# Retention heads: the 80 tail tokens' value block first, state growths among the second z projection

## The chip, the cores and the metric

The kernel runs on one core of a Trainium2 chip. The metric is the device time of one execution in microseconds (us), the median of several runs. One execution was also profiled; every duration below is from it.

## What is computed

One inference step of a two-layer trunk on 528 prompt tokens (16 of them meta tokens) and 8 sample sequences of 8 tokens. Each layer has a retention branch of four heads, a gated recurrent branch, gates and an output projection. The change lies in the retention heads alone:

```python
def retention_chunk(q, k, v, S, log_g):
    ...
    scores = jnp.einsum('blhd,bmhd->bhlm', q, k) * decay[None]
    inner = jnp.einsum('bhlm,bmhe->blhe', scores, v)
    cross = jnp.einsum('blhd,bhde->blhe', q, S) * cross_decay[None, :, :, None]
    S_new = jnp.exp(log_g * L)[None, :, None, None] * S + jnp.einsum(
        'blhd,blhe->bhde', k * state_decay[None, :, :, None], v)
    return inner + cross, S_new
```

Each sample sequence has its own state S (256x512 in f32, 512 KB) per head and layer, which is read, used for `cross`, grown by its 8 tokens and written back.

## The kernel before, in words

The 592 tokens are cut into four blocks of 128 and a tail of 80 (`TAIL`: 16 prompt tokens and the 64 sample tokens). Every matmul in full precision is made of three products of a high and a low part, so each operand is split: ScalarE (ACT) copies the rounded high part (`w_hi`, `vtok_hi`), VectorE (DVE) subtracts to get the low part (`w_lo`, `vtok_lo`).

All engines run programs written out by hand and meet at semaphores. Weights come in units of 512 KB over a ring of four slots: SyncE (SP) issues unit u when unit u - 4 is used up (`unit_done`), ACT and DVE split it (`split_hi`, `split_lo`, lines 398 and 406) three units ahead of its use. Results go to four PSUM banks in turn (`bank`), which ACT or DVE free; the tail's value block has a bank of its own (`v_last`), the samples' output too (`o_last`).

TensorE (PE) runs, for each head: four projections for q and k (units 0 to 3); `values(0)` to `values(3)` (units 4 to 7), each adding two of the eight 128-row steps to all five token blocks of v; between them `keys` (transposes of k) and `cross(0)`, the queries of the first four sample sequences times their states; the z projections `proj 8` and `proj 9`; the score products (five jobs); then `grow(0, 0)`, half of `proj 10`, `grow(0, 1)`, the other half, `grow(1, 0)`; `inner` (four token blocks, 30 matmuls) with `grow(1, 1)` after its second block; the tail's part of the output; `prompt_state(0)`, `cross(1)` with the other four states, `prompt_state(1)`; transposes of the normalised output; `proj 11`; and the product with w_a (units 12 to 15), among which `grow_four` grows the other four states.

`grow(pair, c)` (PE line 1485) makes the new part of two states' half c, from `kst` and `vst`, the stacks of high and low parts of the samples' keys and values. DVE adds it to the decayed state (line 924), and after c = 1 tells POOL (`s_upd`), which stores the two states (line 517), waits for each store to land and loads the next sequence's state into its place (line 512). `cross(1)` waits for these loads.

The stacks go through HBM. In `stacks` SP waits for the split keys (`ktok_ready`), writes them to `k_scr` (three DMAs, line 443), reads them back as `kst` and `kst3` (lines 445, 446), waits for all values (`vtok_ready`), writes `v_scr` (three DMAs, line 449), reads `vst` and `vst3` (lines 451, 452), and waits until everything has landed (`st_in`) before it issues the next weight unit. It does all this behind the load of unit 11. PE waits for `st_in` ahead of `grow(0, 0)`.

In the heads each engine's loop over units i says where its steps stand: DVE updates states at the end of i = 9 and in i = 10, and after the first block's variance.

Of the kernel before, what the change touches and what calls it, by code (L numbers as in the profile page):

```python
# [33 lines left out]
P = 128  # L34
# [8 lines left out]
TB = 5  # L43
# [15 lines left out]
RAW = 4  # L59

# [86 lines left out]
def phases():  # L147
# [3 lines left out]
    r += [(("apart", u), 1) for u in range(3)] + [(("v", j), 0) for j in range(4)] + [(("apart", 3), 1)]  # L151
# [32 lines left out]
def trunk(nc, x_in, w_units, gate_w, packs, final_gain, consts, decay, state_ret,  # L184
# [7 lines left out]
    with ctx:  # L192
# [107 lines left out]
        def sem(name):  # L300
# [20 lines left out]
            "vth_ready", "scm_ready", "sch_ready", "zero_ready", "rest_ready", "scr_in", "st_in"))  # L321
        zt_ready, ktok_ready, vtok_ready, sc_ready = (sem(n) for n in (
# [90 lines left out]
        def _(sp):  # L413
# [24 lines left out]
            def stacks(l, h):  # L438

                hh = l * HEADS + h  # L440
                sp.wait_ge(ktok_ready, hh + 1)
                for n, src in enumerate((ktok_hi, ktok_lo, ktok_hi)):
                    sp.dma_start(k_scr[:, n], src[0:TAIL, 4, :].bitcast(f32)).then_inc(scr_in, 16)
                sp.wait_ge(scr_in, 48 + hh * 96 + 48)
                sp.dma_start(kst[:, :, :].bitcast(f32), stacked(k_scr)).then_inc(st_in, 16)
                sp.dma_start(kst3[0:STACK * TAILP, :].bitcast(f32), k_scr[0:2].rearrange("s p r e -> (s p r) e"))                    .then_inc(st_in, 16)
                sp.wait_ge(vtok_ready, hh + 1)
# [4 lines left out]
                sp.dma_start(vst3[0:STACK * TAILP, :].bitcast(f32), v_scr[0:2].rearrange("s p r e -> (s p r) e"))                    .then_inc(st_in, 16)  # L452
                sp.wait_ge(st_in, hh * 64 + 64)
# [4 lines left out]
            for u in range(RING, UNITS):  # L458
# [11 lines left out]
                if at < HEADS * 16 and at % 16 == 11:  # L470
                    stacks(l, at // 16)
# [9 lines left out]
        def _(pool):  # L481
# [13 lines left out]
            for l in range(0, DEPTH):  # L495
# [7 lines left out]
                for h in range(0, HEADS):  # L503
# [18 lines left out]
                    pool.memset(vst3[STACK * TAILP:P, :].bitcast(f32), 0.0).then_inc(rest_ready, 1)  # L522
# [63 lines left out]
        def _(act):  # L586
# [48 lines left out]
            for l in range(0, DEPTH):  # L635
# [9 lines left out]
                for h in range(0, HEADS):  # L645
# [10 lines left out]
                    for i in range(11):  # L656
# [17 lines left out]
                        if i == 7:  # L674
                            for j in range(TB):
                                if j < 4:
                                    wait_job(act, "R", l, h, ("v", j))
                                else:
                                    wait_job(act, "R", l, h, ("apart", 3))
                                act.activation(vtok_hi[0:BLK[j], j, :], v_bank(j)[0:BLK[j], :], ACT.Copy)\  # L680
                                   .then_inc(vth_ready, 1)
# [1114 lines left out]
```

## Time and profile before

| | |
|---|---|
| runs | 2088.36, 2089.3, 2093.83 us |
| median | 2089.3 us |
| the profiled execution's own time | 2092.4 us |
| its span from the first to the last instruction | 2090.5 us |
| PE busy | 2026.7 us, 97% |
| DVE, ACT, POOL busy | 57%, 34%, 8% |
| mean granted clock of TensorE | 0.993 |

A stage is measured as a stretch of PE's timeline from its first matmul to the first matmul of the next stage. Busy time of PE does not tell a wait exactly, since matmuls are pipelined and their ends are modelled. A row of the windows view begins with the stretch and its length in us, then busy time and instruction count of each engine, then the granted clock, the DMA share and GB/s; its last row sums all stretches asked for. A row of the timeline is start, duration, engine, line, what is written and read, and in brackets the idle time before it. PEld is the loading of weights into the array, which overlaps PE.

The eight heads are the four heads of layer 0 and the four of layer 1. The fourth head is the last of layer 0; its `values(2)` starts at 497.79 us.

### The profile page before, as it was taken

Reading aid. Unit: us, or ns where it says so; the run is one execution under the profiler, and the core shown is the slowest. Engines: PE = TensorE matmul, PEld = TensorE weight load, DVE = VectorE, ACT = ScalarE, POOL = GpSimd, SP = SyncE. Lnnn points to the kernel's source line nnn. Section 1 sums busy time; section 2 is a strip of 40 time slices with the busy share of each in tenths; the row PEclk is TensorE's granted clock in tenths of the full one; section 3 lists DMA queues with packets and bytes.
Section 4 is the critical chain, followed back from the end, with each engine's and each line's share of the span. In section 5 each row is a group of like instructions: output and inputs, shape, how many; then the busy total and the mean of one; then the engine's idle time right before and its main releaser. Section 6 shows DMA issues by size and latency. Waiting matters only on the chain.

```text
span 2090.5 us, 32504 instructions
## 1 busy us (share of the span) xinstructions
PE 2026.7 (97%) x13512; PEld 1866.9 (89%) x13512; DVE 1186.9 (57%) x2021; ACT 715.2 (34%) x1110; POOL 161.5 (8%) x222
## 2 busy tenths in 40 slices
PE   8999999899999999999999999999999999999998
PEld 7878888798799999999987887987987999999997
DVE  7655455464567776424584554645645677753345
ACT  4322222222226665422332222222122366654222
POOL 1020120120200000000001201202102000000000
PEclk9999999999999999999999999999999999999999
DMA  5334443442442212222244334424433422132222
GB/s 206 101 124 159 145 142 97 153 163 85 143 152 84 74 66 101 93 80 72 91 157 152 128 101 154 167 82 148 152 104 127 156 79 79 61 117 81 71 90 79
DMA packets 100833, 241.43 MB, mean 115 GB/s; under 512 B 8622, under 2 KB 48286, under 8 KB 100302
## 3 DMA queue, kind: packets, MB, share of 16 engines
q1 hardware_dynamic: 78446, 149.78, 21.8%
q0 software_dynamic: 22240, 89.57, 12.0%
q8 instruction: 107, 1.75, 0.3%
q14 instruction: 40, 0.33, 0.1%
HBM read 190.13 MB, written 49.18 MB: 114 GB/s over the span
## 4 chain that ended last, share of the span: by engine, by line
PE 66%; DMA 12%; DVE 11%; ACT 3%; DVEq 3%; issue 2%; SPq 2%; ACTq 1%; POOL 1%; POOLq 0%
PE bank L1391 15%; PE bank L1393 15%; PE bank L1392 15%; PE bank L1454 5%; PE bank L1456 4%; PE bank L1455 4%; DMA out_ret_s<-S 4%; DMA w_raw<-in_w_units 2%; PE o_last L1470 2%; DVE w_lo L406 2%; DMA S<-in_state_ret 2%; DVE rr L1273 2%; DVE ct L1211 1%; DMA vst<-v_scr 1%; DVEq L927 1%
## 5 line engine op out<-in xcount | busy, mean ns | idle before, releaser
L1391 PE MATMUL bank<-xn_hi,w_hi 128*128 128x296 f32 x2432 | 728.5, 300 | 6.2 <-DVE w_lo L406 4.9
L1393 PE MATMUL bank<-xn_lo,w_hi 128*128 128x296 f32 x2432 | 726.7, 299 | 0.0
L1392 PE MATMUL bank<-xn_hi,w_lo 128*128 128x296 f32 x2432 | 723.6, 298 | 0.0
L1391 PEld LDWEIGHTS bank<-xn_hi,w_hi 128*128 128x128 f32 x2432 | 457.4, 188 | 12.5 <-DVE w_lo L406 8.0
L1392 PEld LDWEIGHTS bank<-xn_hi,w_lo 128*128 128x128 f32 x2432 | 458.1, 188 | 0.3
L1393 PEld LDWEIGHTS bank<-xn_lo,w_hi 128*128 128x128 f32 x2432 | 456.2, 188 | 0.0
L406 DVE TENSOR_TENSOR w_lo<-w_raw,w_hi 128x1024 fp32r<-128x1024 f32 x245 | 299.1, 1222 | 250.7 <-ACT w_hi L398 244.0
L398 ACT ACTIVATE w_hi<-w_raw 128x1024 fp32r<-128x1024 f32 x245 | 258.5, 1055 | 456.2 <-DMA w_raw<-in_w_units 451.6
L1391 PE MATMUL bank<-oa_hi,w_hi 128*128 128x296 f32 x512 | 154.0, 301 | 0.0
L1393 PE MATMUL bank<-oa_lo,w_hi 128*128 128x296 f32 x512 | 153.2, 299 | 0.0
L1392 PE MATMUL bank<-oa_hi,w_lo 128*128 128x296 f32 x512 | 152.9, 299 | 0.0
L1393 PE MATMUL bank<-ob_lo,w_hi 128*128 128x296 f32 x384 | 115.1, 300 | 0.0
L1391 PE MATMUL bank<-ob_hi,w_hi 128*128 128x296 f32 x384 | 114.5, 298 | 0.0
L1392 PE MATMUL bank<-ob_hi,w_lo 128*128 128x296 f32 x384 | 114.2, 297 | 0.0
L1454 PE MATMUL bank<-w_hi,xn_hi 128*128 128x512 f32 x256 | 102.8, 402 | 2.9 <-DVE rot_k L966 1.4
L1391 PEld LDWEIGHTS bank<-oa_hi,w_hi 128*128 128x128 f32 x512 | 96.3, 188 | 5.8 <-issue 5.8
L1456 PE MATMUL bank<-w_lo,xn_hi 128*128 128x512 f32 x256 | 101.0, 394 | 0.0
L1455 PE MATMUL bank<-w_hi,xn_lo 128*128 128x512 f32 x256 | 100.8, 394 | 0.0
L1392 PEld LDWEIGHTS bank<-oa_hi,w_lo 128*128 128x128 f32 x512 | 96.3, 188 | 0.0
L1393 PEld LDWEIGHTS bank<-oa_lo,w_hi 128*128 128x128 f32 x512 | 96.3, 188 | 0.0
L517 POOL DMA_DIRECT2D out_ret_s<-S x64 | 45.7, 717 | 463.3 <-DVEq L927 291.5
L946 DVE SCALAR_TENSOR_TENSOR zz<-zz,bank 128x296 f32<-128x296 f32 x64 | 29.5, 461 | 83.8 <-ACT zz L653 81.9
(233 smaller groups left out, 3162.5 us busy)
## 6 DMA issues: line engine op xcount, KB each, us to landing
w_raw<-in_w_units SPq DMA_DIRECT2D x216, 512.0 KB, 3.3
S<-in_state_ret POOLq DMA_DIRECT2D x64, 512.0 KB, 4.8
out_ret_s<-S POOLq DMA_DIRECT2D x64, 512.0 KB, 6.0
w_raw<-in_w_units SPq DMA_DIRECT2D x64, 256.0 KB, 3.2
gw<-in_gate_w POOLq DMA_DIRECT2D x8, 896.0 KB, 4.8
vst<-v_scr SPq DMA_DIRECT2D x8, 512.0 KB, 4.1
out_ret_p<-Sp POOLq DMA_DIRECT2D x8, 512.0 KB, 4.0
v_scr<-vtok_hi SPq DMA_DIRECT2D x16, 160.0 KB
```

The source lines that it names most:

```text
L398: act.activation(w_hi[:, n % RING, :], w_raw[:, n % RING, :], ACT.Copy).then_inc(unit_hi, 1)
L406: dve.tensor_tensor(w_lo[:, n % RING, :], w_raw[:, n % RING, :], w_hi[:, n % RING, :].bitcast(f32), SUB).then_inc(unit_lo, 1)
L517: pool.dma_start(dst, S[:, s, :, :]).then_inc(s_out[s], 16)
L946: dve.scalar_tensor_tensor(zz[:, i - 8, a:b], zz[:, i - 8, a:b], 1.0, psum_of("R", name)[:, 0:HALF], ADD, MUL)\
L1273: dve.tensor_tensor_scan(rr[:, t, :], aa[:, t, :], ii[:, t, :], 0.0, MUL, ADD)
L1391: pe.matmul(ps, w_hi[:, slot, cols], x_hi, start=first, stop=False)
L1392: pe.matmul(ps, w_lo[:, slot, cols], x_hi, start=False, stop=False)
L1393: return pe.matmul(ps, w_hi[:, slot, cols], x_lo, start=False, stop=last)
L1454: pe.matmul(ps, left_hi, right_hi, start=first, stop=False)
L1455: pe.matmul(ps, left_lo, right_hi, start=False, stop=False)
L1456: return pe.matmul(ps, left_hi, right_lo, start=False, stop=last)
L1470: ins = pe.matmul(o_last[at:at + QUAD, :], qz[:, c, b * QUAD:b * QUAD + QUAD], S[:, s, c, :], start=(n < 4 and c == 0), stop=(n >= 4 and c ...
```

## The change

The tail's value block is computed first within each `values(u)` (`VALUE_ORDER`), and signals `v_tail_full` by itself. ACT and DVE split it ahead of the others and ahead of unit 10's split. SP's `stacks` is cut into three: `key_rows` behind the issue of unit 9, `key_stack` and `value_stack` behind that of unit 10, and SP no longer waits for the landing (the next head's `key_rows` does). PE waits for `st_in` ahead of `proj 9`. The growths stand: (0, 0) before `proj 9`, (0, 1) between its halves, (1, 0) behind it and ahead of the scores, (1, 1) behind the scores and ahead of `proj 10`. DVE's updates follow them. PE's wait for POOL's memset (`rest_ready`) moves to the tail's output.

```diff
+VALUE_ORDER = (4, 0, 1, 2, 3)
...
-            def stacks(l, h):
-
-                hh = l * HEADS + h
+            def key_rows(hh):
+
                 sp.wait_ge(ktok_ready, hh + 1)
+                if hh:
+                    sp.wait_ge(st_in, hh * 64)
                 for n, src in enumerate((ktok_hi, ktok_lo, ktok_hi)):
                     sp.dma_start(k_scr[:, n], src[0:TAIL, 4, :].bitcast(f32)).then_inc(scr_in, 16)
+
+            def key_stack(hh):
...
-                sp.wait_ge(vtok_ready, hh + 1)
+            def value_stack(hh):
+
+                sp.wait_ge(v_tail_ready, hh + 1)
...
-                sp.wait_ge(st_in, hh * 64 + 64)
...
-                if at < HEADS * 16 and at % 16 == 11:
-                    stacks(l, at // 16)
+                if at < HEADS * 16:
+                    hh = l * HEADS + at // 16
+                    if at % 16 == 9:
+                        key_rows(hh)
+                    elif at % 16 == 10:
+                        key_stack(hh)
+                        value_stack(hh)
...
+                        if i == 7:
+                            act.wait_ge(v_tail_full, hh + 1)
+                            act.activation(vtok_hi[0:TAIL, 4, :], v_last[0:TAIL, :], ACT.Copy).then_inc(vth_ready, 1)
                         split_hi(act, "R", l, h, i)
...
+                        if i == 7:
+                            dve.wait_ge(vth_ready, hh * TB + 1)
+                            dve.tensor_tensor(vtok_lo[0:TAIL, 4, :], v_last[0:TAIL, :],
+                                              vtok_hi[0:TAIL, 4, :].bitcast(f32), SUB).then_inc(v_tail_ready, 1)
                         if i != 9:
                             split_lo(dve, "R", l, h, i)
...
                     project("R", l, h, ("proj", 8), 8)
-                    project("R", l, h, ("proj", 9), 9)
+                    pe.wait_ge(st_in, hh * 64 + 64)
+                    pe.wait_ge(kt_free, hh * 3 + 3)
+                    grow(0, 0)
+                    project("R", l, h, ("proj", 9), 9, (0,))
+                    grow(0, 1)
+                    project("R", l, h, ("proj", 9), 9, (1,))
+                    grow(1, 0)
                     pe.wait_ge(qkl_ready, hh + 1)
...
-                    pe.wait_ge(st_in, hh * 64 + 64)
-                    pe.wait_ge(rest_ready, hh + 1)
-                    pe.wait_ge(kt_free, hh * 3 + 3)
-                    grow(0, 0)
-                    project("R", l, h, ("proj", 10), 10, (0,))
-                    grow(0, 1)
-                    project("R", l, h, ("proj", 10), 10, (1,))
-                    grow(1, 0)
+                    grow(1, 1)
+                    project("R", l, h, ("proj", 10), 10)
...
-                        if i == 1:
-                            grow(1, 1)
                     pe.wait_ge(ktok_ready, hh + 1)
+                    pe.wait_ge(rest_ready, hh + 1)
```

SP's queue before, in the first head, from the load of unit 8 (the first row is units 8 to 11); `w_raw` are weights, `k_scr` and `v_scr` the scratch in HBM, `kst` and `vst` the stacks (with a number: `kst3`, `vst3`):

```order
L469 DMA w_raw<-in_w_units 128x1024 x4
L443 DMA k_scr<-ktok_hi 10x8x256
L443 DMA k_scr<-ktok_lo 10x8x256
L443 DMA k_scr<-ktok_hi 10x8x256
L445 DMA kst<-k_scr 128x2x256
L446 DMA kst_81<-k_scr 64x256
L449 DMA v_scr<-vtok_hi 10x8x512 x2
L449 DMA v_scr<-vtok_lo 10x8x512
L451 DMA vst<-v_scr 128x2x512
L452 DMA vst_95<-v_scr 64x512
L469 DMA w_raw<-in_w_units 128x1024 x8
```

And SP's queue after the change, at the same place:

```order
L479 DMA w_raw<-in_w_units 128x1024 x2
L446 DMA k_scr<-ktok_hi 10x8x256
L446 DMA k_scr<-ktok_lo 10x8x256
L446 DMA k_scr<-ktok_hi 10x8x256
L479 DMA w_raw<-in_w_units 128x1024
L451 DMA kst<-k_scr 128x2x256
L452 DMA kst_81<-k_scr 64x256
L459 DMA v_scr<-vtok_hi 10x8x512 x2
L459 DMA v_scr<-vtok_lo 10x8x512
L461 DMA vst<-v_scr 128x2x512
L462 DMA vst_95<-v_scr 64x512
L479 DMA w_raw<-in_w_units 128x1024 x9
```

The key writes moved ahead of unit 10, the two stacks ahead of unit 11.

DVE before, from the split of unit 11 (`w_lo`) to the first state update (`S`); `zz` is z, `sc` the scores:

```order
L406 TENSOR_TENSOR w_lo<-w_raw,w_hi 128x1024
L946 SCALAR_TENSOR_TENSOR zz<-zz,bank 128x296 x2
L1033 MEMSET sc 128x64 x3
L1034 MEMSET sc 128x192
L1041 TENSOR_TENSOR sc<-bank,dec 128x264 x2
L1041 TENSOR_TENSOR sc<-bank,dec 128x400
L1041 TENSOR_TENSOR sc<-bank,dec 128x272
L1041 TENSOR_TENSOR sc<-bank,dec 128x144
L1046 TENSOR_TENSOR sc<-bank,cst 80x16
L1048 TENSOR_TENSOR sc<-bank,cst 80x4x16
L924 SCALAR_TENSOR_TENSOR S<-S,cst,sums 128x512 x2
L1056 TENSOR_TENSOR sc_lo<-sc,sc_hi 128x1600
```

And DVE after the change, from the same split:

```order
L408 TENSOR_TENSOR w_lo<-w_raw,w_hi 128x1024
L940 SCALAR_TENSOR_TENSOR S<-S,cst,sums 128x512 x2
L962 SCALAR_TENSOR_TENSOR zz<-zz,bank 128x296
L940 SCALAR_TENSOR_TENSOR S<-S,cst,sums 128x512 x2
L962 SCALAR_TENSOR_TENSOR zz<-zz,bank 128x296
L940 SCALAR_TENSOR_TENSOR S<-S,cst,sums 128x512 x2
L1052 MEMSET sc 128x64 x3
L1053 MEMSET sc 128x192
L1060 TENSOR_TENSOR sc<-bank,dec 128x264 x2
L1060 TENSOR_TENSOR sc<-bank,dec 128x400
L1060 TENSOR_TENSOR sc<-bank,dec 128x272
L1060 TENSOR_TENSOR sc<-bank,dec 128x144
```

Three of the four pairs of state updates now stand ahead of the scores, the fourth behind them.

## Rows read from the trace of the kernel before

**Rows 1.** The page, part 1: busy us, share of the span, instructions.
```profile
PE 2026.7 (97%) x13512; PEld 1866.9 (89%) x13512; DVE 1186.9 (57%) x2021; ACT 715.2 (34%) x1110; POOL 161.5 (8%) x222
```

**Rows 2.** Who waited for whom: us in total, times, longest us.
```profile
DVE vo L1078 <- POOL rstd_gn L492: 53.7, 8, 8.0
...
PEld o_last L1470 <- DMA S<-in_state_ret: 36.3, 16, 4.7
...
PE o_last L1470 <- DMA S<-in_state_ret: 20.6, 14, 3.8
...
PEld sums L1485 <- DVE S L924: 15.7, 16, 1.7
```

**Rows 3.** Windows, cross(1) in the eight heads (third head, sum): stretch, length, busy, clock.
```profile
406.29:415.36 9.07, 5.29 (x17) 0.86 (x17) 1.91 (x4) 0.60 (x1) 2.47 (x3) 0.81 0.37 117
...
sum 61.10, PE 40.51 PEld 6.26 DVE 15.31 ACT 4.78 POOL 13.29; mean PE 5.06 PEld 0.78 DVE 1.91 ACT 0.60 POOL 1.66
```

**Rows 4.** Windows, cross(0) in the eight heads: first head, and the sum.
```profile
59.14:60.99 1.85, 1.85 (x17) 0.42 (x16) 1.49 (x2) 0.81 (x1) 0.00 (x0) 1.00 0.51 168
...
sum 14.84, PE 14.84 PEld 3.35 DVE 12.65 ACT 8.75 POOL 0.00; mean PE 1.85 PEld 0.42 DVE 1.58 ACT 1.09 POOL 0.00
```

**Rows 5.** Windows, prompt_state(1) in the eight heads: the sum.
```profile
sum 24.32, PE 24.32 PEld 19.56 DVE 8.24 ACT 4.78 POOL 4.45; mean PE 3.04 PEld 2.45 DVE 1.03 ACT 0.60 POOL 0.56
```

**Rows 6.** Windows, prompt_state(0) in the eight heads: the sum.
```profile
sum 22.57, PE 22.57 PEld 16.54 DVE 0.00 ACT 0.00 POOL 6.45; mean PE 2.82 PEld 2.07 DVE 0.00 ACT 0.00 POOL 0.81
```

**Rows 7.** Windows, second half of proj 10 in the eight heads: the sum.
```profile
sum 33.16, PE 28.18 PEld 26.32 DVE 31.60 ACT 5.55 POOL 0.00; mean PE 3.52 PEld 3.29 DVE 3.95 ACT 0.69 POOL 0.00
```

**Rows 8.** Windows, first half of proj 10 in the eight heads: the sum.
```profile
sum 27.68, PE 27.68 PEld 26.36 DVE 17.36 ACT 20.35 POOL 0.00; mean PE 3.46 PEld 3.30 DVE 2.17 ACT 2.54 POOL 0.00
```

**Rows 9.** Windows, first nine matmuls of inner in the eight heads: the sum.
```profile
sum 24.26, PE 18.88 PEld 12.90 DVE 22.48 ACT 11.80 POOL 11.49; mean PE 2.36 PEld 1.61 DVE 2.81 ACT 1.47 POOL 1.44
```

**Rows 10.** Windows, fourth head: values(3), proj 8, scores, growth (0,0) with half a projection.
```profile
504.79:511.80 7.01, 7.01 (x32) 5.42 (x31) 2.13 (x3) 3.01 (x5) 0.00 (x0) 1.00 0.24 75
511.80:518.32 6.52, 6.52 (x49) 6.52 (x49) 2.55 (x5) 1.01 (x2) 0.00 (x0) 1.00 0.46 137
...
524.84:529.28 4.44, 4.44 (x38) 4.39 (x37) 2.68 (x9) 0.42 (x1) 0.00 (x0) 1.00 0.53 179
529.28:533.17 3.89, 3.89 (x27) 3.48 (x26) 2.24 (x6) 2.69 (x3) 0.00 (x0) 1.00 0.37 146
```

**Rows 11.** Timeline of SP's queue, fourth head: start, us, what is issued.
```profile
517.48 1.54 SPq L449 DMA_DIRECT2D v_scr<-vtok_hi  x2
...
522.51 0.50 SPq L452 DMA_DIRECT2D vst<-v_scr  x1
526.65 0.83 SPq L469 DMA_DIRECT2D w_raw<-in_w_units  x2
```

**Rows 12.** Timeline of ACT, fourth head: tail's high part, split of units 11 and 12.
```profile
512.00 0.59 ACT L680 ACTIVATE vtok_hi<-v_last 80x512 fp32r<-80x512 f32 x1 [0.41 <-PE v_last L1456]
...
518.84 1.05 ACT L398 ACTIVATE w_hi<-w_raw 128x1024 fp32r<-128x1024 f32 x1
...
530.11 1.06 ACT L398 ACTIVATE w_hi<-w_raw 128x1024 fp32r<-128x1024 f32 x1 [4.65 <-DMA w_raw<-in_w_units]
```

**Rows 13.** Timeline of DVE, fourth head: tail's low part, split of unit 11, growth (0,1)'s update.
```profile
513.21 0.68 DVE L1026 TENSOR_TENSOR vtok_lo<-v_last,vtok_hi 80x512 fp32r<-80x512 f32 x1
...
519.92 1.23 DVE L406 TENSOR_TENSOR w_lo<-w_raw,w_hi 128x1024 fp32r<-128x1024 f32 x1 [0.48 <-ACT w_hi L398]
...
536.51 1.40 DVE L924 SCALAR_TENSOR_TENSOR S<-S,cst,sums 128x512 f32<-128x512 f32 x2
```

**Rows 14.** Timeline of POOL: memset of the first head, stores of the third and fourth.
```profile
66.75 0.52 POOL L522 MEMSET vst<- 64x512 f32 x1 [42.10 <-DVEq L1021]
...
397.66 1.43 POOL L517 DMA_DIRECT2D out_ret_s<-S  x2
...
538.57 1.44 POOL L517 DMA_DIRECT2D out_ret_s<-S  x2 [37.10 <-DVEq L927]
```

More of the change, by code:

```diff
@@ L150, in phases @@
         r += halves(("proj", t), 1)
-    r += [(("apart", u), 1) for u in range(3)] + [(("v", j), 0) for j in range(4)] + [(("apart", 3), 1)]
+    r += [(("apart", u), 1) for u in range(3)] + [(("v", j), j // 3) for j in range(4)]
     for t in range(8, 11):
@@ L321, in trunk @@
             "vth_ready", "scm_ready", "sch_ready", "zero_ready", "rest_ready", "scr_in", "st_in"))
+        v_tail_full, v_tail_ready = sem("v_tail_full"), sem("v_tail_ready")
         zt_ready, ktok_ready, vtok_ready, sc_ready = (sem(n) for n in (
@@ L451, in stacks @@
                 sp.dma_start(vst[:, :, :].bitcast(f32), stacked(v_scr)).then_inc(st_in, 16)
[L452 to L453 removed]
+                sp.dma_start(vst3[0:STACK * TAILP, :].bitcast(f32), v_scr[0:2].rearrange("s p r e -> (s p r) e"))\
+                    .then_inc(st_in, 16)
             def stacked(scr):
@@ L521, in _ @@
                     pool.wait_ge(ktok_ready, hh + 1)
-                    pool.memset(vst3[STACK * TAILP:P, :].bitcast(f32), 0.0).then_inc(rest_ready, 1)
+                    pool.memset(vst3[STACK * TAILP:P, :].bitcast(f32), 0.0)
+                    pool.drain().then_inc(rest_ready, 1)
                     for pair in range(S_RING // PAIRED):
@@ L674, in _ @@
                         if i == 7:
[L675 to L680, printed above, removed]
+                            for j in VALUE_ORDER[1:]:
+                                wait_job(act, "R", l, h, ("v", j))
+                                act.activation(vtok_hi[:, j, :], v_bank(j)[:, :], ACT.Copy)\
                                    .then_inc(vth_ready, 1)
@@ L1022, in _ @@
                         if i == 7:
[L1023 to L1029 removed]
+                            for n, j in enumerate(VALUE_ORDER[1:]):
+                                dve.wait_ge(vth_ready, hh * TB + (n + 2))
+                                dve.tensor_tensor(vtok_lo[:, j, :], v_bank(j)[:, :], vtok_hi[:, j, :].bitcast(f32),
+                                                  SUB).then_inc(freed("R", ("v", j)), 1)
                             dve.drain().then_inc(vtok_ready, 1)
                         if i == 9:
+                            grow(1, 0)
                             for j in range(3):
@@ L1089, in gate @@
                                                         MUL, MUL)
-                    variance(0, False)
-                    grow(1, 1)
-                    for j in range(1, 4):
+                    for j in range(4):
                         variance(j, j == 3)
@@ L1505, in values @@
                         wait_unit("R", l, h, 4 + u)
-                        for j in range(TB):
+                        for j in VALUE_ORDER:
                             rows = BLK[j]
@@ L1513, in values @@
                                 k = 2 * u + i
-                                if h == 0 and j == 0:
+                                if h == 0 and j == VALUE_ORDER[0]:
                                     pe.wait_ge(xn_ready, l * KT + k + 1)
@@ L1520, in values @@
                                 done("R", ("v", j), ins)
-                        done("R", ("apart", u), ins)
+                            elif u == 3:
+                                ins.then_inc(v_tail_full, 1)
+                        if u < 3:
+                            done("R", ("apart", u), ins)
                     raw = (xg_hi, xg_lo)
```

19 lines of the change are left out of this document (6 added, 13 removed).

## The prediction

> **What bounds the kernel now.** I read the page's busy times first: TensorE (PE) is busy for 97% of the span [rows 1]. So only what makes PE wait, or makes its instructions longer, can be won. The list of waits [rows 2] names the waits of PE and of its weight loads (PEld; both wait at once, so their figures are not added): cross(1), the second half of the products with the sample states (line 1470), waits for reloaded states (S<-in_state_ret), and the growth products (line 1485) wait for VectorE's update of the states (line 924). Both stand in the retention heads, eight of them. To size them I compared stretches of the timeline that hold the same work: from the first matmul of a stage to the first matmul of the next.
>
> The 16 matmuls of cross(1) take 61.10 us over the eight heads [rows 3], the 16 of cross(0), whose states are there long before, 14.84 us [rows 4]: **46.3 us** of waiting. In the third head the stretch is 9.07 us at a granted clock of 0.81, so part of it ran at the lower of TensorE's levels (1.2 of 2.4 GHz) after PE had idled. The 12 matmuls of prompt_state(1) behind cross(1) take 24.32 us [rows 5], the same 12 of prompt_state(0) ahead of it 22.57 us [rows 6]: **1.7 us**, the same low clock running on. The second half of the third z projection takes 33.16 us [rows 7], the first half 27.68 us [rows 8]: **5.5 us**, since growth (1,0) behind it waits for VectorE. The first nine matmuls of inner, up to growth (1,1), take 24.26 us [rows 9]; at 22.57/96 = 0.235 us a matmul 72 of them are 16.9 us, and a restart behind a growth costs about 0.1 each (0.8): **6.5 us** of waiting for VectorE. Together 60.0 us, 7.5 a head. That is the most that the change can find in these places.
>
> **The change, part by part.** I place its steps in the fourth head, where values(3) runs 504.79 to 511.80 and the first z projection 511.80 to 518.32 [rows 10].
>
> Tail block first. In values(3) the 80 tail tokens are six of 30 matmuls: 7.01/5 = 1.4 us, so they are done at 506.2 instead of 511.8. ScalarE copies them in 0.59 [rows 12], VectorE subtracts in 0.68 [rows 13]: v_tail_ready comes at about 507.6. Both engines were waiting for unit 10's weights there, so nothing stands behind. The four other blocks end up to 1.4 us later each; the first of them is due only when the first z projection starts, and ScalarE reaches it behind the same weights as before. Cost 0.
>
> The stack. From the first v_scr issue (517.48) to the landing of the whole stack, which SP waited for before it issued the next weights (526.65), it takes 9.2 us [rows 11]. Starting at 507.6 it is there at **516.8**. PE now asks for it behind the first z projection, at 518.3: 1.5 us to spare, cost 0. The three key writes go out earlier, between two weight loads, and SP no longer sits on the landing, so units 12 and 13 are issued as soon as their slots are free. In the first head of a layer the keys are late: its values(2) starts at 60.99 [rows 4], the memset that waits for the same signal runs at 66.75 [rows 14], 5.8 us in; three issues of some 0.75 [rows 11] end at 8.1, while unit 10's slot is free at 7.0. Unit 10 is 1.1 us late in two heads; between nothing and 1.1 reaches PE each time, I take 0.6: **1.2 us** in all. (The value stack still meets its time: it waits for the tail block, not for the keys.)
>
> Growths. Their number is the same; each costs PE its pair of matmuls and a restart, wherever it stands. New is what VectorE has in hand there. It splits unit 11 at 519.92 for 1.23 [rows 13], and only then makes growth (0,0)'s update, two instructions of 1.40 together [rows 13]: done at 522.55. A growth with the half projection behind it takes 3.89 [rows 10], of which the half alone is 27.68/8 = 3.46 [rows 8] and the pair 0.43; so PE comes to growth (0,1) at 518.32 + 3.89 = 522.2. It waits 0.35, in eight heads **2.8 us**. Growth (0,1)'s and (1,0)'s updates then have 3.5 us of projection each as cover against 1.40 of work; (1,1)'s runs while PE is in the whole third projection (6.5 us), and so does the scores' split. The scores' five products need a bank back from VectorE, behind (1,0)'s update; bounds are 0 and the 1.40 of that update; I take 0, as four banks are free for the first four jobs.
>
> The reloads. PE's times run on: score (4.44 [rows 10]) ends at about 531.4, growth (1,1) and the third projection at 538.5, inner (30 matmuls of 0.235) at 545.6, tail and prompt_state(0) at 552.3. Growth (1,1)'s update is done near 533.7; the first store of the pair before followed 0.66 behind the update (536.51 + 1.40 to 538.57 [rows 13, 14]), so the last two stores start at 534.4. The longest way from there to the end of cross(1) was the third head's: 397.66 [rows 14] to 415.36 [rows 3], 17.7 us. Even so it would end at 552.1, before cross(1) could end undisturbed (552.3 + 1.85). So the 46.3 and the 1.7 go wholly. With the wait gone, nothing idles PE and the clock stays at its upper level.
>
> The Trainium skill, "TensorE: Matmul & The Clock Gate" (section on the HAM clock gate), says that the slow state is the default and activity lifts it; by it the 1.7 us goes only if no wait of like length takes the place of this one, and without that rule I would leave it in: 2035.0 instead of 2033.3.
>
> What is late next: the transposes behind prompt_state(1) need VectorE's normalised blocks, which today wait for a POOL instruction (53.7 us over eight heads [rows 2]) that stands behind the reload issues. These are over 10 us earlier, so it is free when the variances are.
>
> **Sum.** 60.0 - 2.8 - 1.2 = 56.0 us. The profiled execution took 2092.4 us (span 2090.5) and would take 2036.4; it lies 3.1 above the median, so against the median of 2089.3 I forecast **2033.3 us**, 2.7% less.
>
> **Rivals.**
> - VectorE or ScalarE late in the second projection. Unit 11's load now goes out behind the stack's transfers. If it only starts when they land, it is there at 516.8 + 3.46 (526.65 issued, 530.11 used [rows 11, 12]) = 520.3, and ScalarE wants it at 518.84 [rows 12]: 1.4 us later for VectorE and for growth (0,1), 11 us in all: **2044.5**. The same comes of a bank that comes back 1.4 us late in the scores. For it: everything there hangs on one chain. Against it: SP issues it at 513, and a load needs no more than that 3.46 where nothing is ahead. Chance 0.11.
> - The reloads still collide. Stores and reloads now run beside units 13 and 14. If they take a further 3.4 us (one such load) over the longest way above, cross(1) ends at 555.5 instead of 554.2, 1.3 us a head: **2043.7**. The Trainium skill, "DMA: Bandwidth & Descriptors" (section "Issuing engines are not separate DMA queues"), states that transfers issued from all engines interleave on the same 16 DMA engines, which speaks for it. Against it: the way above is already the longest of the eight, and it held the same kind of company. Chance 0.05.
> - The wait moves to the transposes. If the POOL instruction were late for another reason, the 46.3 would return there: **2079.6**. Against it: its cause is the issue order, which changes. Chance 0.04, half of it within 0.3%.
> - Slower than before. PE now needs the stack 11 us earlier. Each microsecond over 1.5 is paid in every head. If the writes and reads, queued behind unit 10's load and the key stack, took twice their 9.2 us, PE would wait 7.7 us a head, 61.6 in all against the 56.0: **2094.9**; it decides at 17.7 us for the stack. Against it: the 9.2 us were themselves taken behind a weight load and the key stack. Chance 0.03.
>
> **How the numbers follow.** Forecast 0.77. Faster by over 0.3% (about what a measurement of this kernel can tell from no change): 0.77 + 0.11 + 0.05 + 0.02 = 0.95; within: 0.02; slower: 0.03. The range reaches from the whole 60.0 us won, with some 2 us for the runs' spread and a first values block that waits less (2027), to the first two rivals (2045).
>
> **What would show it.** cross(1) near 1.86 us a head and no wait for S<-in_state_ret at all; granted clock 1.00 there. The second half of the third projection like the first, inner 30 matmuls in 7.0 us without a gap. A wait of the growth for line 924's successor of about 0.35 us a head, and none for the stack. PE over 99% busy. If the stretch between the first z projection and the growth shows PE waiting for vst or kst, the stack's term is wrong; if cross(1) still waits, the reloads' is.

## The result and the profile after

| | before | after |
|---|---|---|
| median of the runs | 2089.95 us | 2033.96 us |
| runs from, to | 2088.36 to 2093.83 | 2033.44 to 2036.12 |
| span of the profiled execution | 2090.5 us | 2034.3 us |
| mean granted clock of TensorE | 0.993 | 0.999 |

The ratio of the times is 0.9731, with a 95% interval of 0.9715 to 0.9748: 2.7% faster. The forecast was 2033.3 us. The page, part 1, has PE at 98% of the span with 28.4 us less of busy time than in [rows 1], for the same 13512 matmuls: in the kernel before, waiting also showed as busy time, because the ends of matmuls are modelled, and some matmuls were slow.

```profile
PE 1998.3 (98%) x13512; PEld 1864.3 (92%) x13512; DVE 1187.1 (58%) x2021; ACT 715.6 (35%) x1110; POOL 161.5 (8%) x222
```

The waits of PE alone, three of the seven that the view lists (against [rows 2]; columns: us in total, times, longest). The seven come to 26.5 us; the four left out are 4.9, 4.4, 2.1 and 1.1. The wait for reloaded states (S<-in_state_ret) is gone altogether:

```profile
PE bank L1406 <- DVE w_lo L888: 9.4, 1, 9.4
...
PE v_last L1469 <- DVE xn_lo L927: 3.5, 4, 1.4
...
PE sums L1500 <- DVE S L940: 1.1, 3, 0.6
```

The last of these is the growths' wait for VectorE (now line 940). In the kernel before, PE's own row for it was:

```profile
PE sums L1485 <- DVE S L924: 10.4, 15, 1.3
```

The same stretches as in [rows 3 to 9], in the windows view (stretch, length, busy time and count of PE, PEld, DVE, ACT and POOL, granted clock, DMA share, GB/s). cross(1), third head and the sum of eight; then the sum of prompt_state(1):

```profile
395.26:397.12 1.86, 1.86 (x18) 0.42 (x17) 0.00 (x0) 0.60 (x1) 0.00 (x0) 1.00 0.02 4
...
sum 14.86, PE 14.86 PEld 3.36 DVE 0.00 ACT 4.78 POOL 0.00; mean PE 1.86 PEld 0.42 DVE 0.00 ACT 0.60 POOL 0.00
...
sum 23.19, PE 23.19 PEld 18.47 DVE 8.25 ACT 4.78 POOL 4.45; mean PE 2.90 PEld 2.31 DVE 1.03 ACT 0.60 POOL 0.56
```

The first half of proj 9, now behind growth (0, 0): first, third and fourth head, and the sum. A half without a wait takes 3.46, so the sum holds 30.13 - 27.68 = 2.4 us of waiting:

```profile
82.81:86.69 3.88, 3.54 (x26) 3.30 (x24) 3.00 (x4) 1.47 (x3) 0.00 (x0) 1.00 0.40 135
...
361.51:365.65 4.14, 3.54 (x26) 3.30 (x24) 3.05 (x5) 1.58 (x3) 0.00 (x0) 1.00 0.35 127
500.57:504.25 3.68, 3.54 (x28) 3.30 (x26) 3.00 (x4) 1.16 (x3) 0.00 (x0) 1.00 0.39 142
...
sum 30.13, PE 28.30 PEld 26.42 DVE 24.08 ACT 10.05 POOL 0.00; mean PE 3.54 PEld 3.30 DVE 3.01 ACT 1.26 POOL 0.00
```

And three more sums of eight: the second half of proj 9, proj 10 whole, inner whole (30 matmuls):

```profile
sum 27.68, PE 27.68 PEld 26.32 DVE 13.05 ACT 0.00 POOL 8.85; mean PE 3.46 PEld 3.29 DVE 1.63 ACT 0.00 POOL 1.11
...
sum 53.00, PE 53.00 PEld 53.00 DVE 41.77 ACT 17.25 POOL 17.17; mean PE 6.62 PEld 6.62 DVE 5.22 ACT 2.16 POOL 2.15
...
sum 55.56, PE 55.56 PEld 45.14 DVE 36.66 ACT 24.38 POOL 11.43; mean PE 6.95 PEld 5.64 DVE 4.58 ACT 3.05 POOL 1.43
```

In each of the three PE's busy time equals the length, and the lengths are those of undisturbed work (3.46 us a half; the forecast had 7.0 for inner, and it takes 6.95): nothing is waited for.

What the first half of proj 9 waits for stands in the timelines of ACT and then of DVE, fourth head (idle time before and its cause in brackets). PE ends proj 8 at 500.14; ACT's tanh of it, the split of unit 11 on ACT and on DVE, and growth (0, 0)'s update follow each other with pauses of half a microsecond at most, and the update ends at 504.19, when PE, without a wait, would have been at growth (0, 1) by 500.57 + 3.46 = 504.03:

```profile
500.25 0.42 ACT L669 ACTIVATE zz<-bank 128x296 f32<-128x296 f32 x1 [2.84 <-PE bank L1408]
500.56 1.05 ACT L400 ACTIVATE w_hi<-w_raw 128x1024 fp32r<-128x1024 f32 x1
```

```profile
501.65 1.23 DVE L408 TENSOR_TENSOR w_lo<-w_raw,w_hi 128x1024 fp32r<-128x1024 f32 x1 [0.49 <-ACT w_hi L400]
502.79 1.40 DVE L940 SCALAR_TENSOR_TENSOR S<-S,cst,sums 128x512 f32<-128x512 f32 x2
```

How the stack meets its time, in the fourth head, whose values(2) now starts at 479.59. SP's queue (start, us, what is issued; compare [rows 11]):

```profile
489.51 1.54 SPq L459 DMA_DIRECT2D v_scr<-vtok_hi  x2
...
493.93 0.39 SPq L461 DMA_DIRECT2D vst<-v_scr  x1
494.36 1.43 SPq L462 DMA_DIRECT2D vst<-v_scr  x1
```

The view of the tile vst in this stretch gives the landing of its two reads:

```profile
DMA to landing us min/median/max: 4.0/4.5/5.1
```

The first value row goes out 9.9 us after values(2) begins, as worked out (507.6 - 497.79 = 9.8). The second read is in at 494.36 + 5.1 = 499.5 at the latest, PE asks at 500.14: 0.6 us to spare, where the forecast had 1.5 (in the third head, where the same view has 5.3 us for the longer read, it is 0.5). From the first write issued to the last landing it took some 10 us where the sum had 9.2, and still nobody waited.

POOL in the same head, stores (line 532) and reloads (line 527):

```profile
516.55 1.43 POOL L532 DMA_DIRECT2D out_ret_s<-S  x2
...
523.47 0.71 POOL L527 DMA_DIRECT2D S<-in_state_ret  x1 [0.50 <-issue]
```

The page's part on DMA issues (count, KB each, median us to landing) has for all reloads:

```profile
S<-in_state_ret POOLq DMA_DIRECT2D x64, 512.0 KB, 5.1
```

The last reload is issued at 523.47 and, at the median, in some 5.1 us later, at 528.6. cross(1) starts at 533.85: over 5 us to spare. The tightest is the seventh head: its last reload, issued at 1386.07, took 7.6 us, and cross(1) starts at 1398.38, 4.7 us later. Before, cross(1) was the stretch that waited.

The third of the prediction's rivals had the wait move to the transposes, which need POOL's instruction. In [rows 2] VectorE waited 53.7 us for it, and now:

```profile
DVE vo L1095 <- POOL rstd_gn L507: 9.3, 8, 1.2
```

The stretch of the first transposes behind prompt_state(1) takes 13.4 us in eight heads, and took 13.3 before: nothing moved there.

### The profile page after: what moved, and what is told of

Read it like the earlier page. It is cut to its first block, busy times and chain, and to the rows that moved or that the text cites. A ratio compares the mean times of both kernels' runs of the same rounds, so it can differ in the third digit from the quotient of the medians.

```text
span 2034.3 us, 32511 instructions
## 1 busy us (share of the span) xinstructions
PE 1998.3 (98%) x13512; PEld 1864.3 (92%) x13512; DVE 1187.1 (58%) x2021; ACT 715.6 (35%) x1110; POOL 161.5 (8%) x222
## 4 chain that ended last, share of the span: by engine, by line
PE 77%; DVE 12%; ACT 4%; DMA 2%; DVEq 2%; issue 2%; ACTq 1%; SPq 1%
PE bank L1406 18%; PE bank L1408 17%; PE bank L1407 17%; PE bank L1469 6%; PE bank L1470 6%; PE bank L1471 6%; DVE w_lo L408 2%; DMA w_raw<-in_w_units 2%; DVE rr L1288 2%; DVE ct L1226 2%; PE o_last L1485 1%; ACT rr L793 1%; PE sums L1500 1%; ACTq L792 1%; ACT w_hi L400 1%
```

## The experiments

Each ran on a chip beside the kernel before. Ratios are to that kernel. The edits are to the changed kernel unless told otherwise.

### Is it the growths' place that wins the time?

The growths, PE's and VectorE's part both, back at their old places, everything else as changed (PE's part of the edit):

```diff
-                    grow(0, 0)
-                    project("R", l, h, ("proj", 9), 9, (0,))
-                    grow(0, 1)
-                    project("R", l, h, ("proj", 9), 9, (1,))
-                    grow(1, 0)
+                    project("R", l, h, ("proj", 9), 9)
...
-                    grow(1, 1)
-                    project("R", l, h, ("proj", 10), 10)
+                    grow(0, 0)
+                    project("R", l, h, ("proj", 10), 10, (0,))
+                    grow(0, 1)
+                    project("R", l, h, ("proj", 10), 10, (1,))
+                    grow(1, 0)
...
+                        if i == 1:
+                            grow(1, 1)
```

> Changed kernel with the early tail block, the early stacks and the free SP queue, but with the four growths back at their old places. Theory (the 46 us of cross(1) go only because the states are updated, stored and reloaded earlier): cross(1) still waits about 5 to 6 us a head; only the waits ahead of growth (1,0) and (1,1), 12 us, go: 2076 to 2080 us. Rival (the early stack and SP's free queue carry the gain, the place of the growths does not): 2034 to 2040 us, cross(1) near 1.9 us a head.

Measured: 2081.76 us, ratio 0.9976 (0.9962 to 0.999), a little above the 2076 to 2080 expected. So the early stack alone wins about a quarter of a per cent, and the growths' places, which need the early stack (below), the rest. In its windows cross(1), third head and sum, and then the sum of the first nine matmuls of inner:

```profile
405.89:413.89 8.00, 5.61 (x18) 0.84 (x17) 1.92 (x4) 0.60 (x1) 1.36 (x2) 0.79 0.35 125
...
sum 51.44, PE 34.50 PEld 5.61 DVE 15.33 ACT 4.78 POOL 9.86; mean PE 4.31 PEld 0.70 DVE 1.92 ACT 0.60 POOL 1.23
...
sum 29.40, PE 18.91 PEld 12.87 DVE 24.49 ACT 17.62 POOL 11.49; mean PE 2.36 PEld 1.61 DVE 3.06 ACT 2.20 POOL 1.44
```

cross(1) still waits 36.6 us. The wait in proj 10's second half has gone (27.65 us, against 33.16 in [rows 7]), but what is won there comes back in inner, up from 24.26 [rows 9] to 29.40: PE is only earlier at growth (1, 1), for which VectorE's update of growth (1, 0) is not done sooner. Most of what the trace shows as won stands in cross(1), 9.7 us shorter than in [rows 3]; the next run shows the same, and in what part of it.

The kernel before, with SP's wait for the landing put off to the next head's key rows:

```diff
                 sp.wait_ge(ktok_ready, hh + 1)
+                if hh:
+                    sp.wait_ge(st_in, hh * 64)
...
-                sp.wait_ge(st_in, hh * 64 + 64)
```

> Kernel before in which SP does not wait for the stack's landing before it issues the next weights (the next head's key rows wait for it instead). Theory (the 12 us ahead of growth (1,0) and (1,1) come from unit 12's late arrival, which holds ScalarE and then VectorE): 2078 to 2084 us, cross(1) still waits. Rival (they come from the order of VectorE's own work): 2089 to 2091 us.

Measured: 2084.35 us, ratio 0.9984 (0.9966 to 1.0001). The interval holds 1, so the times alone do not show a gain; what follows is read from the trace. The sums of proj 10's second half, of inner's first nine matmuls and of cross(1):

```profile
sum 27.67, PE 27.67 PEld 26.31 DVE 24.90 ACT 0.77 POOL 0.00; mean PE 3.46 PEld 3.29 DVE 3.11 ACT 0.10 POOL 0.00
...
sum 29.43, PE 18.90 PEld 12.88 DVE 24.50 ACT 17.62 POOL 11.48; mean PE 2.36 PEld 1.61 DVE 3.06 ACT 2.20 POOL 1.44
...
sum 54.87, PE 34.41 PEld 5.58 DVE 15.31 ACT 4.78 POOL 11.89; mean PE 4.30 PEld 0.70 DVE 1.91 ACT 0.60 POOL 1.49
```

This splits the 12.0 us that the prediction found before growths (1, 0) and (1, 1). The 5.5 of the first came from unit 12, which SP issued only after the landing: with SP free they are gone. The other was VectorE's own order at that place, and took 5.2 of them back: both kernels, this one and the one above, take the same 3.68 us in every head there. cross(1) became 6.2 us shorter than in [rows 3], and nearly all of it is PE's busy time in the stretch, 34.41 us against 40.51 (34.50 in the run above). The heads' rows say where: the granted clock of cross(1) was 0.74 to 0.82 in six heads of the kernel before, and is 0.79 to 0.81 in two heads of this kernel and of the one above, 1.00 in the others. Why it fell less often is open.

Only growth (1, 1) back behind inner's second block:

```diff
-                    grow(1, 1)
                     project("R", l, h, ("proj", 10), 10)
...
+                        if i == 1:
+                            grow(1, 1)
```

> Changed kernel with growth (1,1) alone back behind inner's second block. Theory: its update ends about 44.6 us after values(2) begins (36 now), the last two states are stored and reloaded by 57 to 63, cross(1) is due at 54.7: some 4 us a head of waiting for S<-in_state_ret return, 2066 us (2050 to 2085). Rival (the reload has time enough there too): 2034 to 2038 us.

Measured: 2049.82 us, ratio 0.9823 (0.9803 to 0.9842), 16 us less than the expected 2066 and just below its range. The sum of cross(1):

```profile
sum 30.53, PE 23.31 PEld 4.36 DVE 7.79 ACT 4.78 POOL 0.68; mean PE 2.91 PEld 0.55 DVE 0.97 ACT 0.60 POOL 0.09
```

The growth stands 8.8 us later there (proj 10 takes 6.60, the nine matmuls 2.18), against the 5 us that its reload had to spare: PE waits (30.53 - 14.86)/8 = 2.0 us a head. That is less than the difference of 3.8, since cross(1) works on the earlier states first: in the fourth head six of its 16 matmuls have run before it waits. So the place of this one growth is worth 15.7 us of waiting in cross(1), where all four at their old places give 36.6.

The kernel before without the reload of the second four states (that part of the computation is left out: cross(1) and the later updates read the states that are in the slots; the stores stay):

```diff
-                            apart(pool)
-                            load_state(n + S_RING)
+                            pool.sem_inc(slot_again, 1)
...
-                            dve.wait_ge(s_in[s], (hh * (DEC_BATCH // S_RING) + 2) * 16)
+                            dve.wait_ge(slot_again, hh * S_RING + s + 1)
```

> Kernel before with the reload of the second four sample states left out: cross(1) and the later growths use the first four states again, and cross(1) waits for VectorE's update alone. Theory (the wait is worth its whole length and nothing takes its place): cross(1) near 1.86 us a head, 47 us less: 2042 us; the 12 us ahead of growth (1,0) and (1,1) stay. Rival (the wait moves to the transposes that need the normalised blocks): 2060 to 2080 us.

Measured: 2043.88 us, ratio 0.9793 (0.9761 to 0.9825). 45.2 us go with the reload alone, by the interval 37 to 50, against 46.3 + 1.7 found by comparing stretches. Its profiled execution is not the median one (span 2051.3): there the growths waited more than before (41.09 in proj 10's second half), while cross(1) took 14.85. The cause of that stays open.

### Is it the stack's time that allows it?

The tail's block computed and split last, as before; SP's early key rows and the growths' new places stay:

```diff
-VALUE_ORDER = (4, 0, 1, 2, 3)
+VALUE_ORDER = (0, 1, 2, 3, 4)
...
-                        if i == 7:
-                            act.wait_ge(v_tail_full, hh + 1)
-                            act.activation(vtok_hi[0:TAIL, 4, :], v_last[0:TAIL, :], ACT.Copy).then_inc(vth_ready, 1)
```

> Changed kernel with the tail block computed and split last again; stacks still ahead of unit 11. Theory: the tail's low part is ready 15.9 us after values(2) begins instead of 9.9, the stack lands 9.2 later at 25.1, PE waits 4.5 us a head: 2070 us. Rival (SP's order alone is what made the stack early): 2034 to 2038 us.

Measured: 2087.5 us, ratio 0.9998 (0.9985 to 1.0011). The whole gain is gone, and 17 us more than expected. The sums of proj 8 with the wait for the stack behind it, and of the first half of proj 9 (its clock in the first head at the top):

```profile
sum 90.37, PE 53.67 PEld 51.73 DVE 23.57 ACT 13.43 POOL 0.00; mean PE 6.71 PEld 6.47 DVE 2.95 ACT 1.68 POOL 0.00
...
88.16:94.19 6.03, 6.03 (x28) 5.86 (x26) 2.54 (x3) 1.06 (x1) 0.00 (x0) 0.53 0.16 63
...
sum 45.48, PE 44.87 PEld 43.43 DVE 20.39 ACT 8.88 POOL 0.00; mean PE 5.61 PEld 5.43 DVE 2.55 ACT 1.11 POOL 0.00
```

The wait is as expected: proj 8 takes 53.14 us in the changed kernel, so 37.2 in eight heads, 4.7 each. What was not expected is the 15.3 us more in the half behind it (45.48 against 30.13), and its granted clock of 0.53 in the first head: nearly all of it ran at the lower of TensorE's levels (1.2 GHz).

The stack 4.5 us later by another means, the value rows written twice:

```diff
...
-                sp.wait_ge(scr_in, 48 + hh * 96 + 96)
+                sp.wait_ge(scr_in, 48 + hh * 144 + 96)
+                for n, src in enumerate((vtok_hi, vtok_hi, vtok_lo)):
+                    sp.dma_start(v_scr[:, n], src[0:TAIL, 4, :].bitcast(f32)).then_inc(scr_in, 16)
+                sp.wait_ge(scr_in, 48 + hh * 144 + 144)
```

> Changed kernel whose SP writes the three value rows twice, the second time after the first has landed: the stack lands 4.5 us later. Theory (0.4 to 1.6 us to spare, every further us is paid in each head): 3.1 to 3.5 us a head, 2059 us; with unit 11's load late too, up to 1 us a head more, 2067 us. Rival (more to spare than the landings say): 2034 to 2045 us.

Measured: 2070.22 us, ratio 0.9921 (0.9898 to 0.9943), 3 us above the higher of the two expected times. The same two sums, and the fourth head's half of proj 9 ahead of the second:

```profile
sum 77.15, PE 53.67 PEld 51.75 DVE 18.73 ACT 12.72 POOL 0.00; mean PE 6.71 PEld 6.47 DVE 2.34 ACT 1.59 POOL 0.00
...
515.40:520.39 4.99, 4.99 (x27) 4.81 (x25) 2.54 (x3) 1.06 (x1) 0.00 (x0) 0.66 0.27 107
...
sum 40.72, PE 40.04 PEld 38.56 DVE 20.40 ACT 8.88 POOL 0.00; mean PE 5.00 PEld 4.82 DVE 2.55 ACT 1.11 POOL 0.00
```

24.0 us of waiting, 3.0 a head, and again 10.6 more in the half behind it. Two causes could make these: unit 11's load, which SP issues behind the late stack, so that its split and VectorE's update behind it come late; or the clock.

The old stack altogether: both stacks behind unit 11's load, the tail last, SP waiting for the landing, with the growths at their new places (one place of the edit):

```diff
-                    if at % 16 == 9:
-                        key_rows(hh)
-                    elif at % 16 == 10:
-                        key_stack(hh)
-                        value_stack(hh)
+                if at < HEADS * 16 and at % 16 == 11:
+                    stacks(l, at // 16)
```

> The growths stand as in the changed kernel, but the tail block is computed and split last and SyncE writes and reads both stacks behind unit 11's load, as in the kernel before, and waits for their landing. Theory: the stack bounds the growths and lands some 29 us after values(2) begins, where TensorE now asks at 20.6, so each head waits some 8.4 us at growth (0, 0): 8 x 8.4 = 67, that is 2101 us. Unit 11's load stands ahead of the stacks here, so the wait ahead of growth (0, 1) should stay at 0.3 us or less a head; a lower granted clock behind each wait can add up to 10 (2101 to 2111). Rival: the stack's time did not bound the growths, and the new places alone bring the gain: 2034 to 2060 us.

Measured: 2115.8 us, ratio 1.0128 (1.0111 to 1.0145): slower than the kernel before. PE's wait for the stack in the list of waits, and in the windows the sum of proj 8 with that wait, then the third head of the half behind it and its sum:

```profile
PE sums L1485 <- DMA vst<-v_scr: 63.5, 8, 8.5
```

```profile
sum 117.05, PE 53.59 PEld 51.65 DVE 32.58 ACT 21.20 POOL 0.00; mean PE 6.70 PEld 6.46 DVE 4.07 ACT 2.65 POOL 0.00
...
389.45:395.53 6.08, 6.08 (x28) 5.92 (x26) 1.41 (x2) 0.00 (x0) 0.00 (x0) 0.52 0.26 86
...
sum 44.25, PE 44.25 PEld 42.91 DVE 11.25 ACT 0.00 POOL 0.00; mean PE 5.53 PEld 5.36 DVE 1.41 ACT 0.00 POOL 0.00
```

Some 8 us a head of wait (63.9 in all, where 8.4 a head were expected), and 14.1 us more in the halves although unit 11 came early here and no update was waited for (PE's busy time is the length). The clock of 0.52 speaks for the second of the two causes. So neither part of the change does without the other: the new places with the old stack lose 27 us, the new stack with the old places wins 5.

### What makes the half behind a wait longer?

The kernel with the rows written twice, and VectorE's split of unit 11 put behind growth (0, 0)'s update:

```diff
...
                         elif i == 9:
                             grow(0, 0)
+                            split_lo(dve, "R", l, h, 8)
                             silu(i, (0,))
...
-                        if i != 9:
+                        if i not in (8, 9):
                             split_lo(dve, "R", l, h, i)
```

> e4_stack_late together with the edit of e6_split_behind: the value rows are written twice, and VectorE splits unit 11 behind the update of growth (0, 0). e4 cost 24.0 us of waiting at growth (0, 0), and 10.6 us more in the first half of z projection 9 (4.99 us a head in place of 3.68). Theory: these 10.6 us come from VectorE's order: unit 11's load is issued behind the late stack, its split stands ahead of the update, and growth (0, 1) waits for the update. With the split behind the update this half takes 3.5 us a head and the kernel 2070.2 - 8 x 1.5 = 2058 us (2056 to 2060). Rival: the half is longer because the granted clock is low behind a wait of 3 us, or because the load's lateness only moves on: 2066 to 2071 us.

Measured: 2068.52 us, ratio 0.9903 (0.9887 to 0.9918). The rival came true. The first half of proj 9 in the third, fourth and seventh head, and the sum:

```profile
372.14:377.14 5.00, 5.00 (x26) 4.83 (x25) 2.63 (x3) 1.06 (x1) 0.00 (x0) 0.66 0.28 109
514.90:518.34 3.44, 3.44 (x27) 3.27 (x25) 2.60 (x3) 1.06 (x1) 0.00 (x0) 1.00 0.41 162
...
1391.94:1395.41 3.47, 3.47 (x26) 3.30 (x25) 2.63 (x3) 1.06 (x1) 0.00 (x0) 1.00 0.40 157
...
sum 36.86, PE 36.86 PEld 35.51 DVE 21.02 ACT 8.47 POOL 0.00; mean PE 4.61 PEld 4.44 DVE 2.63 ACT 1.06 POOL 0.00
```

Same work, same order, no wait in any of them. Two heads kept the upper level and took 3.44 and 3.47; six fell and took 5.00. The difference is 1.5 us each. The timeline of PE in the third head (start, us, instruction, idle time before it) shows where the clock falls and where it is back:

```profile
371.71 0.50 PE L1504 MATMUL sums<-vst,kst 24*128 24x512 f32 x2 [3.47 <-DMA vst<-v_scr]
...
372.65 0.30 PE L1410 MATMUL bank<-xn_hi,w_hi 128*128 128x296 f32 x1
...
373.57 0.45 PE L1412 MATMUL bank<-xn_lo,w_hi 128*128 128x296 f32 x1
373.82 0.45 PE L1410 MATMUL bank<-xn_hi,w_hi 128*128 128x296 f32 x1
...
376.50 0.30 PE L1412 MATMUL bank<-xn_lo,w_hi 128*128 128x296 f32 x1
376.64 0.30 PE L1410 MATMUL bank<-xn_hi,w_hi 128*128 128x296 f32 x1
```

Matmuls follow each other every 0.14 us at first, then every 0.25, although PE has been at work again for over a microsecond, and at the end every 0.14 again. So it is the clock. With VectorE's order changed, the six slow heads take what nearly all heads took without (4.99 above): while the half is slow, it also covers the late update. The length of the wait alone does not decide it. The second head fell after a wait of 1.8 us (its proj 8 with the wait took 8.44; in the kernel with the rows written twice alone it was 8.28, a wait of 1.6, and it fell too), the fourth and the seventh did not after 2.8. The Trainium skill, "TensorE: Matmul & The Clock Gate" (Part 1: The HAM clock gate), says that throttled is the default and activity releases it; the rows agree in kind, a fall behind idle time and a return in work. What decides between the heads stays open.

### The growths' wait that is left

The changed kernel with that same edit of VectorE's order:

> Changed kernel with VectorE's split of unit 11 moved behind growth (0,0)'s update. Theory: the half projection before growth (0,1) shrinks from 3.68 (4.14 in the third head) to 3.46 us, 2.4 us in all: 2031.5 us. Rival (VectorE is late there for another reason, or the loss comes back at growth (0,1)'s update): 2034 us.

Measured: 2032.93 us, ratio 0.9743 (0.9723 to 0.9763). The sum of the half:

```profile
sum 27.73, PE 27.73 PEld 26.41 DVE 23.32 ACT 8.49 POOL 0.00; mean PE 3.47 PEld 3.30 DVE 2.92 ACT 1.06 POOL 0.00
```

The 2.4 us are gone from the trace. The changed kernel once more, beside it:

> The changed kernel itself, for comparison on the same chip: 2034 us.

It took 2034.18 us, ratio 0.9746 (0.9726 to 0.9765). The 1.25 us between the two medians are about half of what the trace gives, and the intervals overlap: by the times alone the version is not shown to be better, and it is not slower. The first half of proj 9 in this second profiled execution of the changed kernel, fourth head and sum:

```profile
499.63:503.55 3.92, 3.54 (x28) 3.31 (x26) 3.00 (x4) 1.51 (x3) 0.00 (x0) 1.00 0.40 134
...
sum 29.67, PE 28.31 PEld 26.41 DVE 24.03 ACT 9.60 POOL 0.00; mean PE 3.54 PEld 3.30 DVE 3.00 ACT 1.20 POOL 0.00
```

Here the third head takes 3.68 like the others, and the fourth is the long one. So the part above 3.68 comes and goes between executions; the 0.22 us between 3.46 and 3.68, 1.8 in eight heads, is in both.

Last, unit 11's load between the value rows' writes and the value stack's reads:

```diff
...
+                sp.wait_ge(unit_done, u + 2 - RING)
+                sp.dma_start(w_raw[:, (u + 1) % RING, :], w_units[u + 1]).then_inc(unit_in[(u + 1) % RING], 16)
                 sp.wait_ge(scr_in, 48 + hh * 96 + 96)
...
+                if at < HEADS * 16 and at % 16 == 11:
+                    continue
```

> The changed kernel, with unit 11's load issued between the value rows' writes and the value stack's reads, so ahead of the stack in SyncE's queue. Theory: the load lands some 4 us earlier, the split of unit 11 is over before growth (0, 0) ends, and the first half of z projection 9 falls to 3.5 us a head (2 us in all); but the stack's reads now share the DMA engines with 512 KB that came just before them, land some 1 to 2 us later, and TensorE, which had 0.4 to 1.6 us to spare, waits 0.3 to 1.3 us a head: 2034 - 2 + 2 to 10 = 2034 to 2042 us. Rival: both transfers fit into the same time, the stack is not later, and only the gain stays: 2031 to 2032 us.

Measured: 2035.22 us, ratio 0.9744 (0.973 to 0.9759), no difference to the changed kernel. The first half of proj 9, third and fourth head and sum:

```profile
360.69:364.28 3.59, 3.54 (x26) 3.30 (x25) 3.01 (x4) 0.98 (x3) 0.00 (x0) 1.00 0.45 146
499.34:502.87 3.53, 3.53 (x26) 3.29 (x24) 3.00 (x4) 0.91 (x1) 0.00 (x0) 1.00 0.46 149
...
sum 29.20, PE 28.29 PEld 26.40 DVE 24.04 ACT 8.82 POOL 0.00; mean PE 3.54 PEld 3.30 DVE 3.00 ACT 1.10 POOL 0.00
```

Neither expectation held whole. Six heads stay at 3.67 to 3.69, because the load was not what they waited for: ACT splits unit 11 behind the tanh of proj 8's second half, which waits for PE. The third and the fourth head are shorter, but there PE had waited about as much for the stack just before (proj 8 with the wait took 6.69 and 6.74 us, against 6.61), so nothing is won. No head is above 3.69, where the changed kernel had 4.14 in one execution (ACT's split waited 0.35 us for the load there) and 3.92 in the other; one execution of this kernel does not show that the early issue is the reason. With 512 KB ahead of it the stack's second read landed 4.8 us after its issue in the median, against 4.2. Most of that was covered by what it had to spare: proj 8 with the wait took 53.31 us against 53.14.

## Why the prediction was right, by its steps

| term | forecast | measured, spans of the stages |
|---|---|---|
| cross(1) | 46.3 | 61.10 - 14.86 = 46.2 |
| prompt_state(1) | 1.7 | 24.32 - 23.19 = 1.1 |
| growths (1, 0), (1, 1), less the new wait at (0, 1) | 5.5 + 6.5 - 2.8 = 9.2 | 9.0 (proj 8 to the end of inner) |
| unit 10, and everything outside these stretches | -1.2 | -0.2 |
| sum | 56.0 | 56.1 |

Against the kernel before on the same chip the medians differ by 56.0 us, the spans by 56.2. The mechanism was right. That the sum fits to a few tenths of a microsecond is luck: its terms are off by up to 1.0 us and cancel, and in the second comparison, on another chip, the medians differ by 53.7 us (2087.87 and 2034.18).

**cross(1).** Right in size and cause. Two kernels without its wait (this one and the one without the reload) show the stretch at 14.9 us. Not all of the 46.3 was waiting: in the six heads at the low clock PE's busy time in the stretch was 5.3 to 5.7 us, in the two others 3.9, so up to some 9 us (an estimate from these) was slow matmuls behind the wait. It was also safer than it looked: the prediction let the last reload take the longest way seen, 17.7 us, and so had cross(1) end only 2 us behind it. That way contained cross(1)'s own slow matmuls and waits for earlier reloads; the measured room is 5 us in the fourth head.

**prompt_state(1).** The step that took the same 12 matmuls of prompt_state(0) as the base was a little off: at a granted clock of 1.00 they take 2.90 a head behind cross(1), not 2.82. So 1.1 of the 1.7 was won. It stood in the fifth and the eighth head of the kernel before, which took 3.89 and 3.12 us at clocks of 0.71 and 0.91; the third, which the prediction had in view, took 2.88 at 1.00. The other 0.6 stays in every kernel here whose cross(1) does not wait.

**The growths.** The 2.8 us for VectorE's split of unit 11 measured 2.4 in one profiled execution and 2.0 in the other. The chain is as it was told, split, then update, then growth (0, 1), and taking the split out of it took the wait away. What sets its start is not unit 11's load but ACT's tanh ahead of the split; the prediction had the time from its rows, but not this reason. The scores, where the cost was taken as 0, took 0.8 us more in all (36.38 against 35.56). It was not the bank that the prediction had in mind: with growth (1, 1) alone moved away from behind them, and VectorE's update of (1, 0) still ahead of them, they take 35.59. proj 8, with a growth behind it now, took 0.7 us more. These costs were not in the sum; within the 9.0 they are covered by gains that were not in it either, such as proj 10 without a growth in its middle (6.62 us a head against 2 x 3.46).

**The stack.** It starts when it was said to, takes some 10 us where the prediction took 9.2, and arrives 0.6 instead of 1.5 us ahead in the fourth head. That it cost nothing was close.

**Unit 10.** The keys of the first heads are late as worked out. values(2) and values(3) took 0.4 us more in all, not 1.2. The longer wait for VectorE's xn_lo (3.5 us now) is no loss beside it: in these heads values(0) became 2.1 us shorter in all and the keys behind it 1.9 longer.

**The sign that did not come.** PE was to be over 99% busy, and was 98%. The waits that are left stand mostly in other stages (9.4 us of the 26.5 in one place), and no term of the prediction has them.

**The rivals.** The first, unit 11's load late, was there in single heads: 0.5 us in the third and 0.2 in the first, and in the other execution 0.2 in the fourth. The second, reloads that still collide, did not come: in the tightest head 4.7 us are left. Nor did the third (above). The fourth, slower than before, did not come, but its mechanism is real, and its price was too low. With the stack made later PE waits for all of it that is beyond what it had to spare, and then pays the clock on top: 34.5 us for 24.0 of waiting, 54.5 for 37.2, 79.8 for 63.9 (spans of 2068.8, 2088.8 and 2114.1 against 2034.3). At the last of these rates that rival's 61.6 us would have been 77.

## What to carry to other kernels

Measure a wait by the same work elsewhere in the trace: equal stretches gave 46.3 us for cross(1) where the list of waits had 20.6 for PE [rows 2]. When a consumer is moved ahead, look for what it then waits for: here the move pays only with the stack's own shortening, and without it the kernel is slower than before. And count a new wait of PE of two to three us as more than its length: in 14 of 16 heads of two kernels here it cost 1.5 us on top.

## What the runs showed of the hardware

A wait of TensorE of 1.6 to 4.2 us in the middle of dense work was followed, after about a microsecond of matmuls at full speed, by some 3 us at the lower level, where a matmul of 296 columns takes 0.25 us in place of 0.14. That was 1.5 us more in 14 of 16 heads (the two kernels with the rows written twice); two waits of 2.8 us had no such effect, for no reason that the rows show. Behind longer waits the low clock set in sooner and lasted longer: behind 4.1 to 5.1 us (the tail last) the halves took 1.3 to 2.7 us more, and behind 7.2 to 8.5 us the clock was low from the first matmul on (0.52 in the third head's half). And 512 KB put into the queue ahead of the stack's reads let the second read land 0.6 us later in the median (4.8 against 4.2) and delayed what waited for it by 0.2 us in all.
